# Gates projected with their columns standing, odd heads mirrored over the partition halves, and three reorderings in one mixer stage

## The reference

```python
h = rmsnorm(x, mix_norm[l])
p = h @ w_in[l]
u_a, v_a, qkv, z, b_raw, a_raw = jnp.split(p, split_at, axis=-1)
y_a = spatial_gating(gelu(u_a), gelu(v_a), gm_w_s[l], gm_b_s[l], gm_ln_g[l], gm_ln_b[l])  # layer norm of v, 128x128 mix, gate
qkv = silu(causal_dwconv(qkv, dn_conv_w[l]))
q, k, v = jnp.split(qkv, 3, axis=-1)                # q, k: l2norm of each head; 4 heads of 128
beta = sigmoid(b_raw)                               # 4 columns
g = -exp(dn_a_log[l]) * softplus(a_raw + dn_dt_bias[l])   # 4 columns
o = gated_delta_rule(q, k, v, beta, g)              # 4 chunks of 64 tokens, a scan with a 128x128 state per head
y_b = rmsnorm(o, dn_norm[l]) * silu(z)
x = x + concatenate([y_a, y_b], axis=-1) @ w_out[l]
# inside a chunk: decay from cumsum(g); L from k k^T; W = (L + I)^-1 (v - decay * k S);
# o = decay * q S + attn W;   S = S * exp(g_last) + (k decayed)^T W
```

## Time and profile before

| | before |
|---|---|
| median of 3 runs | 1274.63 us (1273.02 to 1275.01) |
| the profiled execution | 1272.23 us, span 1270.4 us |
| PE busy in the span | 1246.6 us (98%) |
| POOL, ACT, DVE busy | 748.0, 600.1, 525.8 us |
| mean granted clock of TensorE | 0.997 |
| the first mixer, from 196.5 us to the first product of `w_out` at 337.65 us | 141.2 us |

### The profile page before, as it was taken

How to read it: one execution, slowest core, us unless ns; L and a number is a source line. 1 busy time by engine, 2 the same in 40 slices (tenths; PEclk the granted TensorE clock), 3 DMA queues, 4 the chain that set the end, 5 groups by cost and what they waited for, 6 DMA issues and landing times.

```text
span 1270.4 us, 22688 instructions
## 1 busy us (share of the span) xinstructions
PE 1246.6 (98%) x9448; PEld 1091.5 (86%) x9448; DVE 525.8 (41%) x808; ACT 600.1 (47%) x786; POOL 748.0 (59%) x190
## 2 busy tenths in 40 slices
PE   8999999999999999999999999999999999999998
PEld 7888888888898888899998888877888898888887
DVE  4233325643533333243533333356767645333333
ACT  7445534323464554486565444444232455544442
POOL 3988870112169888776369888810025424788885
PEclk9999999999999999999999999999999999999999
DMA  7555553224245555554235555523342012555552
GB/s 295 213 191 182 189 204 116 89 100 161 104 151 209 183 188 195 198 191 166 100 134 198 189 183 191 198 100 133 133 166 102 3 37 96 174 200 195 198 187 77
DMA packets 30586, 200.74 MB, mean 158 GB/s; under 512 B 3376, under 2 KB 5296, under 8 KB 6832
## 3 DMA queue, kind: packets, MB, share of 16 engines
q1 hardware_dynamic: 27776, 195.39, 43.2%
q10 hardware_dynamic: 2736, 4.26, 1.0%
HBM read 197.55 MB, written 2.10 MB: 157 GB/s over the span
## 4 chain that ended last, share of the span: by engine, by line
PE 91%; DVE 4%; ACT 2%; issue 1%; POOL 1%; DMA 1%; SPq 0%; POOLq 0%; DVEq 0%
PE psum L335 24%; PE psum L337 12%; PE psum L326 9%; PE psum L328 9%; PE psum L327 9%; PE psum L968 8%; PE psum L981 5%; PE psum L2697 1%; POOL wlo L3046 1%; PE psum L2713 1%; PE psum L2602 1%; PE psum L583 1%; DMA raw<-stream 1%; PE psum L1978 1%; PE psum L2667 0%
## 5 line engine op out<-in xcount | busy, mean ns | idle before, releaser
L3046 POOL TENSOR_TENSOR wlo<-raw,whi 128x2048 fp32r<-128x2048 f32 (+1 forms) x154 | 708.5, 4605 | 402.9 <-ACT whi L296 385.3
L335 PE MATMUL psum<-f_both,whi 128*128 128x512 f32 x1408 | 492.2, 393 | 1.6 <-DVE wlo L681 1.6
L296 ACT ACTIVATE whi<-raw 128x2048 fp32r<-128x2048 f32 x153 | 293.0, 1915 | 240.6 <-PE psum L337 169.4
L337 PE MATMUL psum<-f_both,wlo 128*128 128x256 f32 x1408 | 393.7, 280 | 0.0
L335 PEld LDWEIGHTS psum<-f_both,whi 128*128 128x128 f32 x1408 | 264.3, 188 | 60.2 <-DVE wlo L681 2.1
L337 PEld LDWEIGHTS psum<-f_both,wlo 128*128 128x128 f32 x1408 | 264.5, 188 | 1.5
L326 PE MATMUL psum<-whi,ahi 128*128 128x512 f32 x352 | 137.4, 390 | 0.3 <-POOL wlo L3046 0.3
L328 PE MATMUL psum<-whi,alo 128*128 128x512 f32 x352 | 137.0, 389 | 0.0
L327 PE MATMUL psum<-wlo,ahi 128*128 128x512 f32 x352 | 136.9, 389 | 0.0
L891 DVE TENSOR_TENSOR psum<-psum,arena 128x512 f32<-128x512 f32 x43 | 30.1, 700 | 241.8 <-ACT arena L607 241.7
L968 PE MATMUL psum<-arena,raw 128*128 128x256 f32 x480 | 110.5, 387 | 0.0
(11 more groups left out here) (389 smaller groups left out, 1439.7 us busy)
## 6 DMA issues: line engine op xcount, KB each, us to landing
raw<-stream SPq DMA_DIRECT2D x182, 1024.0 KB, 4.9
con<-consts SPq DMA_DIRECT2D x1, 1184.0 KB, 13.8
x<-x_in SPq DMA_DIRECT2D x1, 1024.0 KB, 5.0
raw<-stream SPq DMA_DIRECT2D x2, 512.0 KB, 7.1
kept_x<-x ACTq DMA_DIRECT2D x1, 1024.0 KB, 3.9
x<-kept_x ACTq DMA_DIRECT2D x1, 1024.0 KB, 4.8
out<-x SPq DMA_DIRECT2D x4, 256.0 KB, 2.0
arena<-gm_w_s ACTq DMA_DIRECT2D x1, 512.0 KB
```

The lines of the kernel that those rows point to most:

```text
L296: nc.scalar.activation(whi[:, slot, :], raw[:, c % RAW, :], ACT.Copy).then_inc(high_made, 1)
L335: nc.tensor.matmul(psum[:, bank, :].rearrange("p (a n) -> p a n", a=2), whi[w], f_both[:, :, k, :], start=k == 0, stop=False, skip_group_c ...
L337: return nc.tensor.matmul(psum[:, bank, 0:TOK], wlo[w], f_hi[:, k, :], start=False, stop=k == KT - 1, skip_group_check=True)
L3046: nc.gpsimd.tensor_tensor(part(wlo[:, slot, :]), part(raw[:, c % RAW, :]), part(whi[:, slot, :]).bitcast(F32), ALU.subtract)\
```

## The change

Five edits, all in the first mixer. `rows_of(c, h)` is `half_rows(c + h)`: tokens of chunk c lie in half c % 2 for even heads and in the other half for odd heads.

1. Gates: `gate_rows` takes the 8 gate columns as the standing operand and moves 256 tokens of the unscaled `h_first` (8 products with 256 moving columns), half of them before and half after the second part of the first projection. DVE multiplies the 8 rows by the scale (`gate_y`), and 8 small products with the identity turn them to tokens, in the mirrored order; they stand behind the first quarter of `W_IN(7)`.
2. `spread_scale` stands behind tile 5 of the first projection instead of behind its end, in bank 4 instead of 7.
3. Mirrored odd heads: `square_sums` has twice as many products of half the size; `turned` keeps its transposes for heads 0 and 2 and uses products with the identity by chunk for 1 and 3; the scan's products alternate over the halves; state sums lie in banks 4 and 5 by the head's parity. DVE's and ACT's copies of a whole half become two each, one per parity.
4. The layer norm of `va` stands within `chunk(3)` between L1326 and the copy of W, the gains of `zg` behind that copy; on PE `mixed` stands before `columns(1, 0)`.
5. `out_tensor` of this mixer does its first chunk in two passes, tiles 2 and 3 last for both halves of the tokens.

```diff
+        "ident_again": i[:, 0:64] == j,
-            for k in range(KT):
-                if k == 4:
-                    turn_half(eng, n, ready, 3)
+            for k in tiles:
                 eng.wait_ge(S["h_high"], 8 * n + k + 1)
...
+                if k == spread:
+                    spread_scale(eng, n, 4)
...
+            for tiles in ([k for k in order if k not in late], late):
+                for m in range(TT):
+                    for k in tiles:
...
+        rows_of = lambda c, h: half_rows(c + h)
+        state_sum = lambda h: bank4(4 + h % 2)[:, h // 2, :]
...
-            scale_row(eng, n, R_mix, 7)
+            scale_row(eng, n, R_mix, 4)
...
+            projected(eng, W_IN(12))
+            nc.vector.tensor_tensor(gate_y, psum[0:8, GATE_ROWS, 0:TOK], R_mix[0:8, :], ALU.mult).then_inc(s("m1_y"), 1)
...
-                nc.vector.tensor_copy(Wb[r, :], psum[r, 2, :]).then_inc(s("m1_wb"), 1)
+                for p in range(2):
+                    r = rows_of(c, p)
+                    nc.vector.tensor_copy(of_parity(Wb[r, :], p), of_parity(psum[r, 2, :], p)).then_inc(s("m1_wb"), 1)
...
-            first_plain_projection(eng, W_IN(6), n, 4 * (STAGES.index(st) - 1), h_first)
-            spread_scale(eng, n, 7)
+            first_plain_tiles(eng, W_IN(6), n, h_first, range(4))
+            turn_half(eng, n, 4 * (STAGES.index(st) - 1), 3)
+            gate_rows(range(4))
+            first_plain_tiles(eng, W_IN(6), n, h_first, range(4, KT), spread=5).then_inc(chunk_used, 1)
+            gate_rows(range(4, KT)).then_inc(chunk_used, 1)
             eng.wait_ge(s("rows_loaded"), 96)
+            eng.wait_ge(S["rms_scale"], scale_at[n + 1])
...
-            project(eng, W_IN(12), plain_tokens, n=8, h=hs, wait=lambda k: eng.wait_ge(S["h_low"], 8 * n + k + 1))
-            project(eng, W_IN(7), plain_columns, h=hs)
+            quarter(eng, W_IN(7), first_scaled, 0, hs)
+            eng.wait_ge(s("m1_y"), 1)
+            for c in range(4):
+                for p in range(2):
+                    mm = nc.tensor.matmul(gates[rows_of(c, p), c // 2, p:8:2], gate_y[:, c * 64:c * 64 + 64],
+                                          const("ident", 8)[0:8, p:8:2], start=True, stop=True)
...
-                for h in range(4):
-                    mm = nc.tensor.transpose(bank4((2, 5)[m])[:, h, :], qkv[:, t0 + h, m * P:(m + 1) * P], const("ident"))
+                for h in (0, 2):
+                    nc.tensor.transpose(to[:, h, :], qkv[:, t0 + h, m * P:(m + 1) * P], const("ident"))
+                for h in (1, 3):
+                    for c in (2 * m, 2 * m + 1):
+                        mm = nc.tensor.matmul(to[rows_of(c, h), h, :], qkv[:, t0 + h, c * 64:c * 64 + 64], const("ident"),
+                                              start=True, stop=True)
...
-            chunk(3)
+            chunk(3, after_r=layer_normed, after_w=gate_gains)
...
+            mixed(0)
+            mixed(1)
             columns(1, 0)
             columns(1, 1)
-            mixed(0)
-            mixed(1)
```

More of the change, by code:

```diff
@@ L1030, in out_tensor @@
                 wait = (lambda k: eng.wait_ge(ready, order[k])) if j == 0 else None
-                tokens_out(SLOT[c], 6 + j % 2, order=list(order), wait=wait).then_inc(chunk_used, 1)
+                if j == 0 and late:
+                    tokens_out_late(SLOT[c], 6, list(order), late, wait).then_inc(chunk_used, 1)
+                else:
+                    tokens_out(SLOT[c], 6 + j % 2, order=list(order), wait=wait).then_inc(chunk_used, 1)
                 if j:
@@ L1081, in build @@
         half_rows = lambda c: slice((c % 2) * 64, (c % 2) * 64 + 64)
+        rows_of = lambda c, h: half_rows(c + h)
+        state_sum = lambda h: bank4(4 + h % 2)[:, h // 2, :]
+        of_parity = lambda v, p: v.rearrange("p (a b d) -> p b a d", b=2, d=P)[:, p, :, :]
         INVERSE_BANK = (0, 3)
         MIXED_BANK = (5, 0)
+        GATE_ROWS = proj_bank(W_IN(12))
+        gates = psum[:, GATE_ROWS, 256:272].rearrange("p (m k) -> p m k", m=2)
+        gate_y = Rm[0:8, 0:2, :].rearrange("p a n -> p (a n)")
         def mix1_scalar(eng, highs, st):
@@ L1095, in mix1_scalar @@
             steps = Steps(eng, "act_step")
-            projected(eng, W_IN(12))
-            eng.wait_ge(s("m1_y"), 1)
-            read(nc.scalar.activation(mh(ba_beta), bank2(proj_bank(W_IN(12)))[:, :, 0:4], ACT.Sigmoid), W_IN(12))
+            eng.wait_ge(s("m1_wturned"), 3)
+            eng.wait_ge(s("m1_y"), 2)
+            read(nc.scalar.activation(mh(ba_beta), gates[:, :, 0:4], ACT.Sigmoid), W_IN(12))
             steps(nc.scalar.activation(ba_abs, ba_y, ACT.Abs))
@@ L1156, in gate @@
                 projected(eng, W_IN(j))
-                zc = zg[:, :, (j - 10) * 256:(j - 10) * 256 + 256]
-                read(nc.scalar.activation(zc, bank2(proj_bank(W_IN(j))), ACT.Silu), W_IN(j))
+                at, made = (j - 10) * 256, bank2(proj_bank(W_IN(j)))
+                nc.scalar.activation(zg[:, :, at:at + P], made[:, :, 0:P], ACT.Silu)
+                for c in range(2):
+                    ins = nc.scalar.activation(zg[rows_of(c, 1), :, at + P:at + 2 * P], made[half_rows(c), :, P:2 * P], ACT.Silu)
+                read(ins, W_IN(j))
             highs.upto(CH[("w_out", 0, 0)])
@@ L1417, in mix1_tensor, with gate_rows @@
             eng.wait_ge(s("masks_loaded"), 16)
-            first_plain_projection(eng, W_IN(6), n, 4 * (STAGES.index(st) - 1), h_first)
-            spread_scale(eng, n, 7)
+            def gate_rows(tiles):
+                c = CH[W_IN(12)]
+                plain_loaded(eng, c)
+                for k in tiles:
+                    eng.wait_ge(S["h_high"], 8 * n + k + 1)
+                    mm = nc.tensor.matmul(psum[0:8, GATE_ROWS, 0:TOK], raw[:, c % RAW, k * 256:k * 256 + 8], h_first[:, k, :],
+                                          start=k == 0, stop=k == KT - 1)
+                return mm
+            first_plain_tiles(eng, W_IN(6), n, h_first, range(4))
[3 more added lines that the diff above has]
+            gate_rows(range(4, KT)).then_inc(chunk_used, 1)
             eng.wait_ge(s("rows_loaded"), 96)
+            eng.wait_ge(S["rms_scale"], scale_at[n + 1])
             for b in range(2):
@@ L1424, in mix1_tensor @@
                 mm.then_inc(s("m1_wturned"), 1)
-            project(eng, W_IN(12), plain_tokens, n=8, h=hs, wait=lambda k: eng.wait_ge(S["h_low"], 8 * n + k + 1))
-            project(eng, W_IN(7), plain_columns, h=hs)
+            first_scaled = lambda slot, bank, h, parts: plain_columns(slot, bank, h, lambda k: eng.wait_ge(S["h_low"], 8 * n + k + 1), parts)
+            quarter(eng, W_IN(7), first_scaled, 0, hs)
+            eng.wait_ge(s("m1_y"), 1)
+            for c in range(4):
+                for p in range(2):
+                    mm = nc.tensor.matmul(gates[rows_of(c, p), c // 2, p:8:2], gate_y[:, c * 64:c * 64 + 64],
+                                          const("ident", 8)[0:8, p:8:2], start=True, stop=True)
+            mm.then_inc(s("m1_wturned"), 1)
+            for part in (1, 2, 3):
+                quarter(eng, W_IN(7), first_scaled, part, hs)
             columns = lambda j, part: quarter(eng, W_IN(j), plain_columns, part, hs)
```

122 lines of the change are left out of this document (76 added, 46 removed).

## The result

The changed kernel takes 1260.67 us (median of 4 runs, 1260.41 to 1261.73), the kernel before 1274.55 us on the same chip (1273.02 to 1275.01): ratio 0.9895, 95% interval 0.9878 to 0.9912, 13.9 us less. The forecast was 1265.5 us with a range of 1261.5 to 1270.

The account below looks back on a forecast made before the run. PE, busy 98% of the span, was taken to bound the kernel. Terms 2.1 + 0.3 - 2.4 + 7.3 + 1.8 = 9.1 us, taken from the median 1274.6, gave 1265.5 us, range 1261.5 to 1270.

Parts of the forecast that it names:

- Start, clock: Start of the first mixer: 2.1 us gained (1.3 to 2.8), 1.7 of it from the slow clock behind 8-column gate products going.
- Start, the smaller terms: Same start: gates fill a 0.56 us wait, scale copied 0.8 us earlier, turning the gates takes 1.1 us.
- The new wait for bank 6: Start of the mixer, behind the transposes: PE waits 0.65 us until DVE has read bank 6.
- Square sums and block products: Both, twice in the mixer: 0.3 us gained (-1.0 to 1.0), with only every second change of half overlapping.
- Turned: Turning of keys and values, with changes of tile shape: 2.4 us lost (1.9 to 3.0).
- Scan: Scan's products alternating over the array halves take half the work time: 7.3 us gained (6 to 8).
- (a): Scan: both row halves on one bank go in turn, `solved` and output stay at 1.01; 1268.9 us, chance 0.1.
- (c): Halves don't overlap at all when products are of different heads: about 0 gain, 1275 us; chance 0.05.
- End: End of the mixer, up to and into `w_out`: 1.8 us gained, 0.2 of it from the two passes.
- T + 19.4: Forecast entry of PE into `w_out`, after gelu; T is the end of `from_state(3)`; before, T + 21.87.
- Rival (b): Four chunks: PE waits on DVE's chain, some 8 handovers cost 3 to 4 us; 1269 us, chance 0.12.
- Rival (d): Slow clock comes back elsewhere, behind tiny products in the first 35 us: up to 1284 us, slower; chance 0.03.

Follow-up runs that it names:

- the two others: The kernel before, unchanged, profiled two more times: 1274.52 and 1274.84 us.
- the kernel with gates alone: The kernel before with only edits 1 and 2 put in, heads not mirrored: 1270.24 us (7 runs), ratio to the kernel before 0.9972.

## Why the prediction was right and wrong

*Start, clock.* Right that the 8-column products cause the fall and that it goes with them (128 columns at the same place, in the same order and with 4.93 for 4.83 us: clock 1.00). Wrong in size: "1.7 us of it are the slow clock" was read from one execution. In the two others, which lie in the middle of the runs, the fall costs 3.4 us. The prediction saw the 2.4 us between the profiled execution and the median and carried them over as a constant to a kernel from which their cause had been removed. This is the larger error, 2.1 us, of which 1.6 are seen as clock in the mixer's start and most of the rest lies behind the mixer. Neither it nor the 1.4 us of the square sums and block products alone would have put the time out of the range (1265.5 less 2.1 is 1263.4, less 1.4 is 1264.1); together, and with 1.3 us of smaller terms, they do. The 11.8 us between the two traces lie inside the 6 to 12 us that the prediction gave its terms (their ends, added up, give 4.5 to 11.9), and the 13.9 between the medians don't. Of the 4.1 us that the gates bring in the medians, 0.85 us is work and some 3.3 us go with the clock.

*Start, the smaller terms.* Turning the gates 0.56 us where 1.1 was taken, at the lower end of 0.55 to 1.9; the row of like form (L1492, 0.034 a record) would have given it. The new wait for bank 6 was 0.17 and not 0.65, which gained nothing: gates, tiles and transposes on PE took 0.5 us longer than reckoned, each with 0.1 to 0.2 us where the shape changes (1.82 for 1.73, 1.92 for 1.73, 1.02 for 0.87), and DVE was on time.

*Square sums and block products.* The term that was mis-sized: 0.3 forecast, 1.7 measured, and outside the ends given (-1.0 to 1.0). "Only every second change overlaps" is false: products in runs of two overlap as well as by turns, 0.98 us for 32 records; it takes runs of 4 (1.38) and 8 (1.73) to lose it. Square sums at 1.03 were below the 1.1 to 1.5 given, and block products, now behind products of their own shape, take 0.98 for 1.08.

*Turned.* -2.4 forecast, -2.2 measured; 0.6 of it goes when the transposes of a turning stand together, so changes of shape cost about what was taken.

*Scan.* 7.3 forecast, 7.3 measured, and 7.3 to 7.6 us come back when the heads are not mirrored. Rivals (a) and (c) fall with it. `solved` and the output, whose products in both row halves write different partitions of one bank, take 0.58 in place of 1.01 us.

The page "TensorEngine Tiling (Array Packing)" of the Trainium skill, section "Restrictions and Gotchas", says that different row tiles cannot access the same PSUM bank simultaneously. These rows differ from it for row halves that write different partitions. State sums write all partitions from either half, and wherever both halves take part in them here they stand in two banks: what they would take in one, no run shows.

*End.* T + 19.4 forecast, T + 19.32 measured, with gelu last. Edit 4 is worth 1.8 us. The 0.2 us came (11.86 to 11.59), but not by edit 5 alone: with edit 4 in place the low tiles come in time even without it. The timelines show why. When gelu ends, DVE is idle in the changed kernel, and in the kernel before it is still at the low parts of the turned output, 0.4 us longer.

*Rival (b)* did not come: the copies of W come in time in the first three chunks and cost 0.05 us in the last. *Rival (d)*, the clock falling elsewhere, came in the profiled one of seven executions of the kernel with gates alone, 6.0 x 0.28 = 1.7 us, and that execution is the slowest of them by 1.8. The changed kernel's two profiled executions have a clock of 1.00 in all 4 us windows from 218 to 242 us, and its eight runs of two comparisons lie between 1260.41 and 1261.73 us. None of the seven profiled variants of the changed kernel has a lower clock in those windows either.

## What to carry to other kernels

Look at the granted clock during and behind every stretch of products that move few columns; let the narrow operand stand and the long one move, or move more columns than are needed, since PE paid nearly as much for 8 columns as for 128 (4.83 and 4.93 us). When an effect of one profiled execution is to be subtracted, look first at how far that execution stands from its median: a mechanism that varies from run to run may be the difference. Products in separate halves of the array overlapped here if neighbours in the program were in different halves; a change of tile shape cost 0.15 to 0.2 us, so gather like shapes.

## What the runs showed of the hardware

- 32 records with 8 moving columns took 4.83 us, with 128 moving columns 4.93; behind the first the granted clock of a 3.6 us window was 0.50 to 0.53 in all three traces, behind the second, in one trace, it stayed at 1.00.
- The fall behind one and the same program varies: 3.6 us at 0.53 in one execution, in two others 12 us of windows at about 0.85, 0.50 and 0.75; it cost 1.7 to 3.4 us.
- 32 records of 64 columns, form 128*64: 0.98 us with the halves strictly by turns and in runs of two products per half, 1.38 in runs of four, 1.73 in runs of eight.
- Two row halves writing different partitions of one bank: 8 records of 128 columns 0.58 us, against 1.01 in one half.
